# Hybrid diffusion trunk on one core: the sum of the first two branches' gated tiles moves from GpSimd to VectorE

## The reference, cut to what matters

```
gate_pool, gate_att, gate_ssd = split(sigmoid(h @ w_gate + b_gate), 3)
merged = gate_pool * (o_pool @ wb_pool) + gate_att * (o_att @ wb_att) + gate_ssd * (o_ssd @ wb_ssd)
x = x + g1 * (merged @ w_out)
h2 = rmsnorm(x) * (1 + sc2) + sh2        # then the ConvFFN on h2
```

## Time and profile before

| | |
|---|---|
| time, median of 3 runs | 1328.78 us (1327.65 to 1329.33) |
| profiled execution, its own time | 1328.28 us |
| its span | 1326.5 us |
| TensorE busy | 1296.1 us, 98% of the span |
| VectorE busy | 1086.6 us, 82% |
| ScalarE busy | 652.9 us, 49% |
| GpSimd busy | 164.9 us, 12% |
| mean granted clock of TensorE | 0.996 |
| chain of work that ended last | TensorE 75%, VectorE 14%, ScalarE 6%, issue 3% |

### The profile page before, as it was taken

The page is one execution under the profiler, slowest core; times in us unless marked ns, Lnnn a source line. Parts: engine busy times, 40 slices in busy tenths (PEclk is TensorE's granted clock), DMA queues, the critical chain, the costliest instruction groups (busy, mean ns, idle before and its releaser), DMA issues.

```text
span 1326.5 us, 20238 instructions
## 1 busy us (share of the span) xinstructions
PE 1296.1 (98%) x7634; PEld 1242.6 (94%) x7634; DVE 1086.6 (82%) x2038; ACT 652.9 (49%) x1058; POOL 164.9 (12%) x158
## 2 busy tenths in 40 slices
PE   7999999999999999999999999999999999999997
PEld 5999889998999999999999988899999899999997
DVE  6899888678887989899968998877878889999533
ACT  5643555644556454543375335546455654545332
POOL 0076000001220000000103900000032000000010
PEclk9999999999999999999999999999999999999999
DMA  9566345333352444457735562553235344444441
GB/s 363 190 222 231 120 154 193 122 104 112 117 184 94 147 159 143 162 178 265 239 112 191 200 205 77 187 191 106 86 122 195 96 143 144 160 143 155 143 125 54
DMA packets 58641, 210.00 MB, mean 158 GB/s; under 512 B 6704, under 2 KB 9136, under 8 KB 57008
## 3 DMA queue, kind: packets, MB, share of 16 engines
q1 hardware_dynamic: 56512, 199.71, 45.1%
q0 software_dynamic: 2032, 9.00, 2.1%
HBM read 205.01 MB, written 3.67 MB: 157 GB/s over the span
## 4 chain that ended last, share of the span: by engine, by line
PE 75%; DVE 14%; ACT 6%; issue 3%; DMA 1%; SPq 1%; DVEq 0%; ACTq 0%; POOLq 0%
PE acc L967 22%; PE acc L968 22%; PE acc L969 22%; DVE wl L1719 2%; DVE gates L1944 1%; DVE cv L1900 1%; DVE junk_late L1808 1%; PE mix L1127 1%; DVE ee L2030 1%; DMA head<-in_whead_dram 1%; PE mix L1222 1%; ACT wh L1310 1%; PE mix L1155 1%; DVE hl L1724 1%; ACT hh L1335 1%
## 5 line engine op out<-in xcount | busy, mean ns | idle before, releaser
L967 PE MATMUL acc<-hh,wh 128*128 128x384 f32 x1519 | 517.8, 341 | 1.3 <-DVE hl L1724 0.7
L969 PE MATMUL acc<-hh,wl 128*128 128x384 f32 x1519 | 507.9, 334 | 0.0
L968 PE MATMUL acc<-hl,wh 128*128 128x384 f32 x1519 | 507.7, 334 | 0.0
L1719 DVE TENSOR_TENSOR wl<-raw,wh 128x1024 fp32r<-128x1024 f32 (+1 forms) x276 | 341.4, 1238 | 69.7 <-ACT wh L1310 68.6
L1310 ACT ACTIVATE wh<-raw 128x1024 fp32r<-128x1024 f32 (+1 forms) x276 | 287.0, 1041 | 135.8 <-PE acc L969 135.5
L967 PEld LDWEIGHTS acc<-hh,wh 128*128 128x128 f32 x1519 | 285.1, 188 | 13.8 <-issue 8.0
L968 PEld LDWEIGHTS acc<-hl,wh 128*128 128x128 f32 x1519 | 285.2, 188 | 2.4
L969 PEld LDWEIGHTS acc<-hh,wl 128*128 128x128 f32 x1519 | 285.1, 188 | 0.0
L1900 DVE SCALAR_TENSOR_TENSOR cv<-acc,prm,cv 128x1 f32<-128x1 f32 (+1 forms) x416 | 153.7, 411 | 9.2 <-ACT cv L1473 1.9
L969 PE MATMUL acc<-ah,wl 128*128 128x384 f32 x352 | 117.6, 334 | 0.0
L967 PE MATMUL acc<-ah,wh 128*128 128x384 f32 x352 | 117.6, 334 | 0.0
(11 more groups left out here) (302 smaller groups left out, 1709.1 us busy)
## 6 DMA issues: line engine op xcount, KB each, us to landing
raw<-in_wstream_dram SPq DMA_DIRECT2D x248, 512.0 KB, 3.6
rawm<-in_wstream_dram SPq DMA_DIRECT2D x80, 512.0 KB, 4.3
raw<-in_wstream_dram SPq DMA_DIRECT2D x32, 448.0 KB, 3.4
head<-in_whead_dram SPq DMA_DIRECT2D x8, 1024.0 KB, 15.8
crow_late<-in_cvec_rows_dram POOLq DMA_DIRECT2D x2, 1024.0 KB, 6.6
crow<-in_cvec_rows_dram POOLq DMA_DIRECT2D x2, 1024.0 KB, 5.3
out_y_dram<-yt SPq DMA_DIRECT2D x3, 384.0 KB, 2.4
x<-in_xs_dram SPq DMA_DIRECT2D x1, 1024.0 KB, 7.6
```

What stands on the lines that cost most here:

```text
L967: mm(out, sh, mhi, start=start, stop=False)
L968: mm(out, sh, mlo, start=False, stop=False)
L969: return mm(out, sl, mhi, start=False, stop=stop)
L1719: tt(wl[:, s, 0:n], raw[:, raw_slot(u), 0:n], wh[:, s, 0:n].bitcast(F32), ALU.subtract).then_inc(lo_done, 1)
```

## The change

The eight additions per layer leave GpSimd's program. VectorE does each of them right behind the gate product of tile 8+j, with a wait for that product's own completion, and signals `mg_done` itself. The wait on `mg_done` in the third branch stays. In the changed program a line number is 6 lower from GpSimd's steps to the function `branch`, and 3 lower behind the added lines.

```
--- before.py
+++ after.py
@@ -783,12 +783,6 @@
                         k = u - MIX0 - SLOT_S - 2
                         pool.wait_ge(st_done, count(l, 4, 2 + k))
                         pool.dma_start(news[l, k], end_state[k]).then_inc(st_out, 16)
-                    if BRANCH0 + 5 <= u < BRANCH0 + 9:
-                        for j in (2 * (u - BRANCH0 - 5), 2 * (u - BRANCH0 - 5) + 1):
-
-                            pool.wait_ge(gb_done, count(l, 24, KT + j))
-                            nc.gpsimd.tensor_tensor(gates[:, j, :], gates[:, j, :], gates[:, KT + j, :], ALU.add) \
-                                .then_inc(mg_done, 1)
                     if u == LATE_ROWS - 2:
 
                         pool.wait_ge(qk_done, count(l, 2 * HEADS, 2 * HEADS - 1))
@@ -1943,6 +1937,9 @@
                     dve.wait_ge(g_done, count(l, 24, 23))
                 stt(out=gates[:, j, :], in0=gates[:, j, :], scalar=1.0, in1=acc[g % BANKS][:, 0:T],
                     op0=ALU.add, op1=ALU.mult).then_inc(gb_done, 1)
+                if b == 1:
+                    dve.wait_ge(gb_done, count(l, 24, j))
+                    tt(gates[:, jj, :], gates[:, jj, :], gates[:, j, :], ALU.add).then_inc(mg_done, 1)
                 if b == 2:
 
                     dve.wait_ge(gb_done, count(l, 24, j))
```

More of the change, by code:

```diff
@@ L785, in _ @@
                         pool.dma_start(news[l, k], end_state[k]).then_inc(st_out, 16)
[L786 to L791, removed]
                     if u == LATE_ROWS - 2:
```

## The result

| | before | changed |
|---|---|---|
| time, median of 22 runs each | 1328.63 us | 1330.49 us |
| lowest and highest | 1327.32, 1333.01 | 1329.37, 1332.94 |
| ratio, 95% interval | | 1.0013 [1.0007, 1.0019] |
| span of the profiled execution | 1326.5 us | 1328.6 us |

The changed kernel is 1.9 us slower (0.9 to 2.5 by the interval). 1330.2 was forecast, in a range from 1327.9 to 1332.0, and "within 0.2%".

What follows compares the result with a forecast made beforehand. TensorE, 98% busy, bounds the kernel and waits on VectorE's chain. Per layer 2.36 - 1.68 = +0.68 us, +1.4 us for both, gives 1329.7 from the profiled execution; set 0.5 higher for the median: 1330.2 us, range 1327.9 to 1332.0.

Steps and rivals of the forecast that it cites:

- VectorE's chain without a gap: Third branch to first OUT unit: VectorE has no slack, so its time moves TensorE one for one.
- The early four at nothing: Units 4 and 5: four additions per layer fit into VectorE's waits, including 2.65 us before the SSD norm; cost nothing.
- 2.36 us for the late four: Units 6 and 7: four additions lengthen VectorE's chain by 1.18 us per unit, 2.36 us per layer.
- 1.68 us given back: Units 6 and 7: VectorE's two `lo` and one addition, slowed beside GpSimd's additions, regain 1.68 us per layer.
- the rule's full block: Units 6 and 7: the skill's exclusive blocking would mean 4.1 us for four additions, against 1.68 seen; chance 0.05.
- The waits of TensorE: First OUT unit, both layers: waits for `ml` grow from 0.44 and 0.46 to about 1.1 us each.
- The rival of the clock: Behind the norm gaps: one more gap at the low clock costs 1.75 us, giving 1332.0; chance 0.10.
- The lower end: First OUT unit, both layers: the wait for `ml` disappears, 0.9 us less, 1327.9; chance 0.05.

Runs made afterwards that it cites:

- two further ones: Changed kernel with one more VectorE addition behind each sum of tiles 4 and 5, none on GpSimd: 1334.23 us, a second time 1334.21 us.
- the two moves: Kernel before, tile 12's gate product moved ahead of the SSD norm, `lo` of the 11th BRANCH unit behind the last low parts: 1327.34 us, again 1326.97.

## Why the prediction was right

- **Where the time goes.** VectorE's chain without a gap from the first product of unit 6 to the last low parts, passed on one for one: right. 0.70 more on VectorE, 0.67 on TensorE's path; with GpSimd's additions left on, 1.33 and 1.35; with two further ones, 1.16 and 1.18.
- **The early four at nothing**: right, +0.02 us per layer when done alone. The norm's wait stayed; it even reads 2.99 us and not 2.65, since the `lo` of unit 5, no longer slowed, ends earlier.
- **2.36 us for the late four**: right; the new rows are 0.58 and 0.48 us apart, as those of the third branch are.
- **1.68 us given back**: right in size and cause. Without any sums both `lo` fall to 1.22 us, and with additions put back on GpSimd they rise to 1.85 again. Products with one input in PSUM ran at 0.55 us beside GpSimd in every run. What I wrote against the rule's full block was wrong, as shown above: it is a full block, but only for what is left of the instruction that came first.
- **The waits of TensorE**: 1.1 us forecast, 1.11 and 1.13 measured. No new wait came in the third branch.
- **The time**: that the median lies within 0.3 us of 1330.2 is partly luck. The mechanism gave 1.35 us of the 1.9; the rest, whose source is open, happened to be small.
- **The rival of the clock** was mis-sized. I took 1.75 us per norm gap from a count of matmuls in 4 us. The distances give 0.4 to 1.1: matmuls missing in a window are time lost only where TensorE would not have waited for tiles. Behind the wait for `ml` the same fall does cost 1.6 us. That a median would hide most of the clock did not hold in full: the changed kernel's executions have the lower mean clock, 0.9947 against 0.9960, and the half microsecond above 1.35 fits that.
- **The lower end**, 0.9 us for the wait for `ml` gone, was mis-sized too: the run without sums shortens the path by 1.78 us. I had read the idle time as the price of a wait.

## What to carry to other kernels

Before moving work off an engine that seems to be in nobody's way, look at what it shares with the engine that takes the work: here 1.68 of 2.36 us came back, and the busy shares (12% and 82%) tell neither number. Which of two contending engines pays is decided by which instruction starts first, where the starts are 0.16 us or more apart; at 0.02 us it came out both ways. Place work by the gaps of the engine that the bottleneck waits for: four of eight equal additions were free, and four cost, because VectorE waits for a third engine between the first four and the chain that TensorE waits for, and no such wait follows the other four. For effects of about a microsecond, compare the distance between two fixed events on the bottleneck, which repeated to 0.04 us, while medians needed some 20 runs for an interval of 1.6 us.

## What the runs showed of the hardware that was not expected

- A wait of TensorE that reads 0.44 us cost 0.88: 0.61 start to start, and 0.27 in three late starts behind it.
- Of two instructions on VectorE and GpSimd that both read two tiles from SBUF, the second lost what was left of the first, less 0.14 us (0.58 of 0.72, 0.86 of 1.00). With starts 0.01 to 0.02 us apart VectorE lost 0.86 us in one kernel and nothing in another.
- Kernels whose matmuls are the same run at different mean clocks, by the mean over their executions: 0.9960 before, 0.9947 changed, 0.9937 with the two moves.
- A wait of 1.74 us in the middle of dense matmuls was followed by the 1.2 GHz level in one execution and not in another of the same kernel (stretch 74.83 and 73.24 us). Waits of 0.44 and 1.1 us never were. This puts a step of 1.6 us on top of a price of one for one. The Trainium skill ("TensorE: Matmul & The Clock Gate", What's actually happening) has the chip watch activity on a window that does not restart with the kernel, which fits a cost that differs from run to run.
- The same fall of the clock cost 1.6 us behind the wait for `ml`, but 0.4 to 1.1 us behind a norm gap.
